# A two-row projection computed as weighted sums on VectorE behind the attention, in place of matmuls behind the gated scan

## The reference, cut to what matters

```
s   = silu(stack([c, c_ctx]))            # 2 x 1024
ada = s @ ada_w                          # 2 x 6144: shift, scale, gate, shift, scale, gate
h   = rms_norm(x, g) * (1 + scale + b_scale) + (shift + b_shift)
```

## Time and profile before

| | us |
|---|---|
| median of 3 runs (4560.31 to 4571.77) | 4562.99 |
| the profiled execution | 4572.53 |
| its span | 4570.8 |

### The profile page before, as it was taken

The page is one execution under the profiler, slowest core; times in us unless marked ns, Lnnn a source line. Parts: engine busy times, 40 slices in busy tenths (PEclk is TensorE's granted clock), DMA queues, the critical chain, the costliest instruction groups (busy, mean ns, idle before and its releaser), DMA issues. The chain is left out here.

```text
span 4570.8 us, 48008 instructions
## 1 busy us (share of the span) xinstructions
PE 3763.4 (82%) x17093; PEld 2428.5 (53%) x17093; DVE 1523.2 (33%) x3680; ACT 1077.4 (24%) x2188; POOL 1013.3 (22%) x911
## 2 busy tenths in 40 slices
PE   7899998997989999999997938967755836765996
PEld 3545776763445666665684425654445835332442
DVE  1012223321532433535431220054476547142001
ACT  0023333321322333323323420021112101110111
POOL 0000002321331333333432440001302534110110
PEclk9999998998999999999998967988877858877998
DMA  3243213247421111111114321362334520444996
GB/s 103 75 124 92 80 40 106 86 147 244 153 97 38 45 50 54 38 47 41 56 43 190 124 101 56 91 165 84 108 83 124 175 92 24 172 165 144 318 318 225
DMA packets 423952, 516.34 MB, mean 113 GB/s; under 512 B 71954, under 2 KB 327482, under 8 KB 423731
## 3 DMA queue, kind: packets, MB, share of 16 engines
q1 hardware_dynamic: 390131, 473.04, 31.3%
q10 hardware_dynamic: 28992, 23.65, 1.6%
q0 software_dynamic: 4608, 16.78, 1.4%
HBM read 378.70 MB, written 134.68 MB: 112 GB/s over the span
## 5 line engine op out<-in xcount | busy, mean ns | idle before, releaser
L622 PE MATMUL hgrn_ps_w<-xT,hgrn_ring 128*128 128x512 f32 x1152 | 507.6, 596 | 0.0
L594 POOL TENSOR_TENSOR hgrn_queries<-hgrn_qd,hgrn_pair_decay 128x640 f32<-128x640 f32 x192 | 285.6, 1506 | 415.0 <-PE hgrn_ps_a L673 198.5
L622 PEld LDWEIGHTS hgrn_ps_w<-xT,hgrn_ring 128*128 128x128 f32 x1152 | 217.0, 192 | 251.7 <-issue 251.6
L1139 PE MATMUL end_ps_z<-end_w,end_yT 128*128 128x512 f32 x768 | 338.1, 600 | 4.4 <-ACT end_yT L1088 2.4
L618 PE MATMUL hgrn_ps_w<-hgrn_ring,xT 128*128 128x256 f32 x1536 | 337.8, 379 | 0.0
L618 PEld LDWEIGHTS hgrn_ps_w<-hgrn_ring,xT 128*128 128x128 f32 x1536 | 289.0, 190 | 38.2 <-issue 0.5
L1139 PEld LDWEIGHTS end_ps_z<-end_w,end_yT 128*128 128x128 f32 x768 | 146.6, 193 | 185.7 <-issue 178.7
L774 DVE COPY_PREDICATED hgrn_scores<-hgrn_mask,hgrn_ps_s 128x128 f32<-128x128 uint32 x192 | 48.5, 297 | 469.0 <-issue 466.7
L346 PE MATMUL gla_bg_ps<-gla_bg_w,xT 128*128 128x256 f32 x768 | 187.6, 397 | 4.6 <-DMA gla_bg_w<-in_w_in_ab_dram 4.6
L346 PEld LDWEIGHTS gla_bg_ps<-gla_bg_w,xT 128*128 128x128 f32 x768 | 150.6, 200 | 38.0 <-issue 10.8
L872 ACT ACTIVATE hgrn_k_tok<-hgrn_ps_a 128x256 f32<-128x256 f32 x84 | 32.3, 384 | 548.8 <-PE hgrn_ps_a L648 548.8
(11 more groups left out here) (575 smaller groups left out, 6743.6 us busy)
## 6 DMA issues: line engine op xcount, KB each, us to landing
expw_wg<-in_exp_w_gate_dram SPq DMA_DIRECT2D x16, 2048.0 KB, 10.6
expw_wu<-in_exp_w_up_dram SPq DMA_DIRECT2D x16, 2048.0 KB, 16.2
expw_wd<-in_exp_w_down_dram SPq DMA_DIRECT2D x16, 2048.0 KB, 21.8
gla_bg_w<-in_ada_w_dram SPq DMA_DIRECT2D x24, 1024.0 KB, 5.3
hgrn_ring<-in_w_in_c_dram SPq DMA_DIRECT2D x36, 512.0 KB, 4.0
end_gt<-gate_l SPq DMA_DIRECT2D x16, 768.0 KB, 7.2
hgrn_ring<-in_w_in_c_dram SPq DMA_DIRECT2D x12, 1024.0 KB, 5.4
hgrn_o<-hgrn_o_stage SPq DMA_DIRECT2D x192, 64.0 KB, 2.6
```

The source lines that it names most:

```text
L594: pool.tensor_tensor(queries[:, d, s, :].rearrange("p (b a c) -> p b a c", b=POINTS, a=PC), q, f, ALU.mult).then_inc(queries_done, 1)
L622: last = pe.matmul(bank[:, :], wt[:, k, 0:P], xT[:, k, part * BANK:(part + 1) * BANK], start=(k == 0), stop=(k == KB - 1))
L1139: made = pe.matmul(ps_z[h][:, :], yT[:, k, :], w[:, k, h * BANK:(h + 1) * BANK], start=(k == 0), stop=(k == NB - 1))
```

## The change

`dilated_attention` gets `sT`, the weights and the output `ada`. The 24 units are kept. For each, SP loads 1 MB of weights (128 x 8 x 256) into one of three buffers. DVE multiplies each of the 8 blocks by the 128 values of `sT` that belong to its partitions and adds it to `acc` (L1573 the first block, L1575 the others): 128 x 256 products, for both rows in the first 8 units and for row 0 alone in the other 16, 256 products in all, three in each step after `move_out`, so in steps 0 to 84 three and in step 85 the last. There is a `drain` on DVE before each product of row 0. PE then sums over the 128 partitions with a column of ones (L1531: one matmul of 512 or 256 columns a unit), ACT moves the row out of a PSUM bank of its own at the head of a step, and SP stores it. That bank is taken from the background, which has 3 instead of 4. The job behind the scan goes.

```diff
                 pe.matmul(ps[n][0:AH, 0:VEC], rb[:, :], bk[:, n * VEC:(n + 1) * VEC], start=True, stop=True).then_inc(made, 1)
-def dilated_attention(nc, tag, qT, kT, vpad, vectors, attn, jobs):
+def dilated_attention(nc, tag, qT, kT, vpad, vectors, attn, jobs, sT, ada_w, ada):
...
     KP = VPAD + SEQ + VPAD
     HEADS = AH // 2
     LEAD = 6
+    ADA_W = 256
+    ADA_UNITS = 6 * D // ADA_W
+    BOTH_ROWS = 2 * D // ADA_W
     with ExitStack() as ctx:
         sb = lambda n, s, d=F32: ctx.enter_context(nc.sbuf_tensor(f"{tag}_{n}", s, d))
         sem = own_semaphores(nc, ctx, tag)
...
         names = ("consts", "scored", "biased", "p_done", "p_turned", "p_moved", "o_made", "o_moved")
         consts, scored, biased, p_done, p_turned, p_moved, o_made, o_moved = (sem(n) for n in names)
         stored = [sem(f"stored{n}") for n in range(3)]
-        bg = Background(sb, sem, pbank, jobs, HEADS * ST, 3, 4, 3, lead=LEAD)
+        w_ada = sb("w_ada", [P, 3, KB, ADA_W])
+        acc, ones, row = sb("acc", [P, 2, 2, ADA_W]), sb("ones", [P, 1]), sb("row", [1, 2, 2, ADA_W])
+        ps_a = pbank("ps_a")
+        ada_loaded, ada_stored = [sem(f"ada_loaded{b}") for b in range(3)], [sem("ada_stored0"), sem("ada_stored1")]
+        weighted, summed, row_moved = (sem(n) for n in ("weighted", "summed", "row_moved"))
+        bg = Background(sb, sem, pbank, jobs, HEADS * ST, 3, 3, 3, lead=LEAD)
         block = ctx.enter_context(nc.Block())
+        def rows_of(u):
+            return 2 if u < BOTH_ROWS else 1
+        def due(u):
+            return unit_ends[u] // 3 + 2
+        PRODUCTS = [(u, kb, r) for u in range(ADA_UNITS) for kb in range(KB) for r in range(rows_of(u))]
+        unit_ends = [n for n, (u, kb, r) in enumerate(PRODUCTS) if kb == KB - 1 and r == rows_of(u) - 1]
+        def products_in(g):
+            return range(3 * g, min(3 * g + 3, len(PRODUCTS)))
+        unit_due = {due(u): u for u in range(ADA_UNITS)}
         def table_of(d, t):
             if d == 0:
...
                 else:
                     sp.dma_start(attn[d, :, cols].rearrange("(p t) c -> p t c", t=TILES), mine).then_inc(stored[d], 16)
+            def load_ada(u):
+                wait(sp, weighted, u - 2)
+                src = ada_w[:, u * ADA_W:(u + 1) * ADA_W].rearrange("(k p) n -> p k n", p=P)
+                sp.dma_start(w_ada[:, u % 3, :, :], src).then_inc(ada_loaded[u % 3], 16)
+            def store_ada(u):
+                sp.wait_ge(row_moved, u + 1)
+                n = rows_of(u)
+                sp.dma_start(ada[0:n, u * ADA_W:(u + 1) * ADA_W].rearrange("(a r) c -> a r c", a=1), row[:, u % 2, 0:n, :]).then_inc(ada_stored[u % 2], 16)
             def late(g):
                 j, s = g // ST, g % ST
...
             sp.wait_ge(consts, 1)
             load(0)
             load(1)
+            load_ada(0)
+            load_ada(1)
+            load_ada(2)
             for g in range(LEAD):
                 bg.transfer(sp, g)
             for g in range(HEADS * ST):
                 bg.transfer(sp, LEAD + g)
+                if g + 1 in unit_due and unit_due[g + 1] + 3 < ADA_UNITS:
+                    load_ada(unit_due[g + 1] + 3)
+                if g - 2 in unit_due:
+                    store_ada(unit_due[g - 2])
                 if g > 2:
                     late(g - 3)
             for g in range(HEADS * ST - 3, HEADS * ST):
                 late(g)
             bg.end(sp)
+            for b in range(2):
+                sp.wait_ge(ada_stored[b], 8 * ADA_UNITS)
             for d in range(3):
                 sp.wait_ge(stored[d], 16 * STORES[d] * HEADS)
...
                 pool.memset(k[:, b, 0:VPAD], 0.0)
                 pool.memset(k[:, b, VPAD + SEQ:KP], 0.0)
                 pool.memset(tab[:, b, :, :], 8 * NEG)
+            pool.drain()
+            pool.memset(ones[:, :], 1.0)
             pool.drain()
             pool.memset(ident[0:1, 0:1], 1.0).then_inc(consts, 1)
...
                         last = pe.matmul(ps_o[:, h * AE:(h + 1) * AE], pT[:, s % 2, h, c, :], v[:, b, v_block(d, t) + c, h * AE:(h + 1) * AE],
                                          start=(c == 0), stop=(c == n - 1))
                 last.then_inc(o_made, 1)
+            def total(u):
+                n = rows_of(u)
+                pe.wait_ge(weighted, u + 1)
+                wait(pe, row_moved, u)
+                pe.matmul(ps_a[0:1, 0:n * ADA_W], ones[:, :], acc[:, u % 2, 0:n, :], start=True, stop=True).then_inc(summed, 1)
             pe.wait_ge(consts, 1)
             for g in range(LEAD):
...
                     score(g + 2)
                 if g:
                     values(g - 1)
+                if g in unit_due:
+                    total(unit_due[g])
                 bg.multiply(pe, LEAD + g)
             values(HEADS * ST - 1)
...
                 dve.drain()
                 dve.tensor_scalar(shift[:, s % 2, :], stage[:, s, P:P + 2], -0.125, None, ALU.mult).then_inc(biased, 1)
+            def weigh(u, kb, r):
+                if kb == 0 and r == 0:
+                    dve.wait_ge(ada_loaded[u % 3], 16 * (u // 3 + 1))
+                    wait(dve, summed, u - 1)
+                mine, w, s = acc[:, u % 2, r, :], w_ada[:, u % 3, kb, :], sT[:, kb, r:r + 1]
+                if kb == 0:
+                    last = dve.tensor_scalar(mine, w, s, None, ALU.mult)
+                else:
+                    last = dve.scalar_tensor_tensor(out=mine, in0=w, scalar=s, in1=mine, op0=ALU.mult, op1=ALU.add)
+                if kb == KB - 1 and r == rows_of(u) - 1:
+                    last.then_inc(weighted, 1)
             def move_out(g):
                 dve.wait_ge(o_made, g + 1)
                 dve.tensor_copy(stage[:, g % ST, 0:P], ps_o[:, 0:P]).then_inc(o_moved, 1)
...
                 bias(g)
                 if g > 1:
                     move_out(g - 2)
+                for n in products_in(g):
+                    if PRODUCTS[n][2] == 0:
+                        dve.drain()
+                    weigh(*PRODUCTS[n])
             move_out(HEADS * ST - 2)
             move_out(HEADS * ST - 1)
...
                 wait(act, o_made, g - 1)
                 act.activation(pT[:, s % 2, :, 0:n, :], ps_t[:, :].rearrange("p (h c q) -> p h c q", h=2, q=P)[:, :, 0:n, :], ACT.Copy).then_inc(p_moved, 1)
+            def move_row(u):
+                n = rows_of(u)
+                act.wait_ge(summed, u + 1)
+                wait(act, ada_stored[u % 2], 16 * (u // 2))
+                act.activation(row[:, u % 2, 0:n, :], ps_a[0:1, 0:n * ADA_W].rearrange("p (r c) -> p r c", c=ADA_W), ACT.Copy).then_inc(row_moved, 1)
             for g in range(LEAD):
                 bg.move(act, g)
             for g in range(HEADS * ST):
+                if g - 1 in unit_due:
+                    move_row(unit_due[g - 1])
                 exps(g)
                 if g:
                     move(g - 1)
...
                 Job(CHANNEL, xT, SEQ, w, 3 * A, 256, 2, qb),
                 Job(CHANNEL, xT, SEQ, w, 4 * A, 256, 2, kb),
                 Job(TOKEN, xT, SEQ, w, 5 * A, 256, 4, vb),
-            ])
+            ], sT, ada_w_2[0], ada)
             low_rank_scan(nc, "gla", 4, B // 4, qb, kb, vb, low, gla_gate_up[0], gla_gate_bias[0], gla_o, 1 / 16, scale, [
                 Job(TOKEN, xT, SEQ, w, 5 * A + B + 2 * RANK, 256, 6, gate_l0),
-                Job(TOKEN, sT, 2, ada_w_2[0], 0, 256, 24, ada),
             ])
         close_layer(nc, "end0", x[0], x1, xT, gla_o, gate_l0, gla_norm[0], w_out_ab[0], ln_gain[0], ln_bias[0],
                     B // 4, alpha, attn=attn, attn_heads=AH)
```

## The result

| | before | changed |
|---|---|---|
| median of 18 runs each, us | 4571.34 | 4578.9 |
| ratio, 95% interval | | 1.0018 [1.0011, 1.0026] |
| span of the profiled execution, us | 4570.8 | 4580.9 |

What follows compares the result with a forecast made beforehand. The prediction took PE to bound both the attention and the scan's projection part. Scan -54, partition sums +13.8, products +36 and attention start +9.5 summed to +5.3, against the median 4563 giving 4568 us, range 4532 to 4606.

Steps and rivals of the forecast that it cites:

- matmuls gone from the scan: Behind the gated scan, 192 projection matmuls of 0.43 us go from PE: -82.6 us.
- longer waits in the scan: In the scan, PE's waits for scaled and moved keys lose 1.7 us of cover, 12 times: +20.5 us.
- clock in the scan: In the scan, longer waits bring about four more slow stretches at half clock: +8 us, between 0 and +18.
- partition sums on PE: In the attention, 24 matmuls on PE sum the partitions, 8 of 512 columns and 16 of 256: +13.8 us.
- products before the bias: In the attention, DVE's 256 products between values copy and next bias make PE wait: +36 us, ends 0 and +55.
- start of the attention: At the attention's start, three 1 MB loads ahead of the first background stores delay ACT and PE: +9.5 us, 0 to 15.
- I leave the sum as it is: In the 24 attention steps with a partition sum, the products' +36 us total was left uncorrected for DVE's extra room.
- rival B: In the attention, short PE pauses lower the clock to 0.91, 40 us more less 7 hidden: 4601, slower; chance 0.15.
- if the granted clock leaves 1.00 in its middle: Sign for the attention: the prediction is wrong if the granted clock leaves 1.00 in the middle of that stage.
- A: Rival, attention: DVE's products fit before the bias is needed, so the 36 us are gone: 4532, faster; chance 0.18.
- D: Rival, scan: waits move ACT and DVE work into the next chain, the 20.5 doubles: 4588, slower; chance 0.10.
- C: Rival, loads in the attention: the start costs nothing, or loads are late once more: 4558 or 4573; chance 0.12.

Runs made afterwards that it cites:

- the experiment: Changed kernel with DVE's three products moved right after the bias, ahead of the copy of the values: 4544.53 us, ratio 0.9954 to the kernel before.
- the three kernels with an unchanged attention stage: The changed kernel (4578.9 us), it with the old projection also kept behind the scan (4629.05), and it with the scan's background spread unevenly (4543.13).
- the kernel with all three edits: Changed kernel with products right after the bias, first loads behind the first stores, scan background placed where PE waits: 4503.74 us, ratio 0.9854 to before.

## Why the prediction was right

It gave 4568 for the runs shown then, 5 above their median, and called the 0.3% band the likeliest; the change measured +8. The direction of each term and its rough size came out of the mechanism. That the net is within 3 us is luck: the scan gave back 5.5 more than forecast and the attention cost 6.9 more, and the two errors cancelled. By its steps:

| term | predicted | found | from |
|---|---|---|---|
| matmuls gone from the scan | -82.6 | -82.6 | 192 fewer; places of 8, 6, 6 records |
| matmuls beside them | 0 | about -6 | the two traces, below |
| longer waits in the scan | +20.5 | +17.4 | 36.3 less 18.9 |
| PE's other waits in the scan | 0 | +3 | the stage's first queries and weights |
| clock in the scan | +8 | about +7 | slow stretches while PE works: 24.0 less 16.6 |
| partition sums on PE | +13.8 | about +20 | below |
| products before the bias | +36 | about +28 | below |
| start of the attention | +9.5 | +10.2 | timelines at the start |
| clock in the middle of the attention | 0 | about +7 | windows below |

**The scan.** The moved-key waits came as said (15 forecast, 14.7 found). The key waits fell short (24 and 21.6): the three long ones grew by 5.05 - 3.33 = 1.72, as worked out, while of the three short ones two grew by about 1 and one hardly (mean 1.45, then 2.14). A term was missing: the removed matmuls had only two columns on the weight side, and they had also slowed their neighbours. In the trace of before:

```profile
1104.89 0.70 PE L1764 MATMUL gla_ps_o<-gla_v_in,gla_scores 128*128 128x256 f32 x2
1105.43 0.59 PE L1766 MATMUL gla_ps_o<-gla_state,gla_queries 128*128 128x256 f32 x2
1105.86 0.59 PE L1764 MATMUL gla_ps_o<-gla_v_in,gla_scores 128*128 128x256 f32 x2
```

The pair that follows the two-column matmuls takes 0.54 to the next, the pair after it 0.43. Adding up the two traces from each record's start to the next one's, the other matmuls of the scan take about 6 us less at full clock in the changed kernel. With this the sum closes: -82.6 - 6 + 17.4 + 3 + 7 is -61, and the edges of the stage give 1 back, against -59.5.

**The products.** The sizes of single waits were right (0.36 and 0.80; two-row steps at the start of the kernel with later loads show 0.64 and 0.45, where the mean was taken as 0.53), the number of them was not: 50 where I had 71. The step that failed is "I leave the sum as it is". A partition sum gives the background place in front of the scores 0.5 to 0.9 us more, as long as the wait itself, so that of the 71 steps about 20 lost theirs. The feared cost beside it, ACT copying the row ahead of the exponentials, was nothing. Against this a wait costs PE a little more than its brackets show: 574.42 - 573.03 = 1.39 where the same pair is 0.53 apart without a wait, so 0.86 with [0.80]; 50 times 0.06 is 3 us. That makes 28, and the experiment, which also takes part of the clock's loss away, shows 63.4 - 33.4 = 30 against the mean of the three kernels with an unchanged attention stage (66.2, 59.9, 64.2).

The pitches taken from other stages held. Two products a drain apart took 1.04 with 0.48 for one, so 0.56, and three with one drain among them 1.44, so 0.56 + 0.40. The Trainium skill, "VectorE: DVE Perf Modes", section "The DRAIN you can't avoid", has the next operation start only when the pipe is empty, and adds at once that an operation that is not held starts earlier, which the prediction left out. The undrained pair starts 0.08 before the one in front ends, as in rows 8, so the trace goes by that exception.

**The start.** Size and mechanism were right. ACT's third background move came at 276.98 (276 forecast), the first exponential at 281.73 (281).

**The clock in the attention.** Here the forecast had nothing and rival B had 40 us; the truth was a mild form of B. By the prediction's own sign, "if the granted clock leaves 1.00 in its middle", this step was wrong. PE's 20-us windows stayed at 1.00 but for a few; this one is part of the middle:

```profile
576.00:586.00 10.00, 10.00 (x46) 7.50 (x46) 4.26 (x14) 4.13 (x12) 0.00 (x0) 0.83 0.32 105
```

Four windows of 20 us stood at 0.90 to 0.93, together some 7 us lost. The Trainium skill, "TensorE: Matmul & The Clock Gate", section "A second HAM failure mode: psum-queue depth-cycling", describes short pauses that make the clock swing. The trace agrees in kind: a few stretches fell with no pause over 0.8 us near them. In size it does not: in a hundred microseconds of the same pauses (370 to 470) the clock was 1.00. Of the four executions with these pauses, the changed kernel had four slow stretches there, the others three, one and none. Of the five without them none had any; this row is of the kernel with all three edits:

```profile
280.00:680.00 400.00, 398.60 (x1976) 268.60 (x1975) 204.05 (x785) 152.49 (x500) 0.00 (x0) 1.00 0.40 120
```

**The partition sums.** In that kernel the attention is 24.0 us longer than before, of which 3.3 are at the start (279.79 - 269.35 less 7.14) and 0.7 are waits for the shift behind it. What is left, some 20, is the price of the 24 sums. In the timeline of the changed kernel:

```profile
559.42 1.10 PE L1523 MATMUL att_ps_o<-att_v,att_pT 128*128 128x64 f32 x8
560.46 0.59 PE L1531 MATMUL att_ps_a<-att_acc,att_ones 128*1 128x256 f32 x2
560.98 2.43 PE L346 MATMUL att_bg_ps<-att_bg_w,xT 128*128 128x256 f32 x10
```

The sum of 256 columns stands 0.52 before the next matmul, not 0.43 (0.66 at the low clock, at 576.66), and the values in front of it take 1.04 where they take 0.94 with no sum behind them (564.98 to 565.92). Counted over the trace the 24 sums themselves are 16 us, and the matmuls on both sides of them 4. It is the same effect as in the scan. The step that failed here is that both prices took the pitch from inside a row of like matmuls, 0.215 a record. That pitch leaves out what a matmul of one or two weight columns costs its neighbours. That the narrow weight side is the cause is read from these rows; no run tests it by itself. In the two stages the error is about 6 us each, in opposite directions.

**How the attention closes.** Added up over the two traces, PE's idle time is 35 us more, the sums and their neighbours 20, the 3 us hidden behind the brackets, and the clock 9 where PE works. That is 67, less 1 at the stage's edges, against 66.2 measured. Three kernels with the same attention stage differ by 6 us in it (66.2, 59.9, 64.2). That too is the clock: slow stretches while PE works cost 11.3, 4.8 and 11.0 us there, and most of what is left of the difference is idle time. Why the clock fell in one execution and not in another, no run shows.

The rivals. A fell: the products do not fit where they stand, though they fit easily 2 us earlier. D fell: no wait for the keys grew by more than the lost cover (the wait for the stage's first queries, 4.0 then 6.5, lies ahead of both chains). C fell: the loads cost what was worked out.

## What to carry to other kernels

Work given to an engine that is idle three quarters of the time still costs what it exceeds the spare time by, where it stands between the event that the bottleneck produces and the answer that it waits for. The same instructions placed before the idle engine's own wait left 0.7 us of waits in two steps. So read on which side of its wait the idle time lies, and write the added work there. Background matmuls are also cover: when some of them go, those that stay belong in front of the waits (25 us here without the change, 35 with it). A bulk load goes into the queue behind the small stores that someone needs back. And a matmul with a narrow weight side is priced with its neighbours.

## What the hardware showed beyond that

- Next to a matmul with one or two weight columns each neighbour stood about 0.1 us further from the next one: 0.54 for 0.43 in the scan, 1.04 for 0.94 in the attention.
- After the same wait of 3.33 us the clock fell in one case and not in another; after 5.05 it was low in every case looked at (at 834, 918 and 998).
- Pauses of 0.3 to 0.8 us in every second step gave full clock for hundreds of microseconds, and then 0.83 for ten.
- Three loads of 1 MB held the issuing queue 7.25 us, so that not only their own packets were in front of the next store but its issue came late: it was issued 7.66 later and landed about 10 us later than before.
